# Sums of squares moved to VectorE, the norms' work in another order, and a pointwise product in three passes

## What is computed

```python
x = layer_norm(ALPHA * x + gt1 * y, ln1_g, ln1_b)          # "l1"
h = x * (1.0 + sc2) + sh2
f = jnp.square(jax.nn.relu(h @ w_ff1)) @ w_ff2
x = layer_norm(ALPHA * x + gt2 * f, ln2_g, ln2_b)          # "l2"
# second block, even layer, for x and for the context:
h = rmsnorm(x, e_norm) * (1 + scale) + shift               # "en"
a_val, a_glu, a_gate, b_val, b_gate = split(h @ e_w_in)
u = a_val * sigmoid(a_glu)
u = silu(layernorm(dwconv(u, a_conv_w) + a_conv_b))
y_a = (u @ a_pw_w + a_pw_b) * silu(a_gate)                 # the pointwise product
y_b = fourier_mix(b_val, b_fw) * silu(b_gate)
x = x + gate * (concat(y_a, y_b) @ e_w_out)
```

## Time and profile before

| | |
|---|---|
| median of 3 runs (lowest, highest) | 2692.74 us (2689.59, 2699.69) |
| the profiled execution's own time, and its span | 2691.15 us, 2689.3 us |
| busy: TensorE, VectorE | 2496.9 us (93%), 1397.6 us (52%) |
| busy: GpSimd, ScalarE | 732.4 us (27%), 610.2 us (23%) |
| mean granted TensorE clock | 0.966 of full speed |

### The profile page before, as it was taken

How to read it: one execution, slowest core, us unless ns; L and a number is a source line. 1 busy time by engine, 2 the same in 40 slices (tenths; PEclk the granted TensorE clock), 3 DMA queues, 4 the chain that set the end, 5 groups by cost and what they waited for, 6 DMA issues and landing times.

```text
span 2689.3 us, 29003 instructions
## 1 busy us (share of the span) xinstructions
PE 2496.9 (93%) x11544; PEld 1946.7 (72%) x11544; DVE 1397.6 (52%) x1577; ACT 610.2 (23%) x882; POOL 732.4 (27%) x490
## 2 busy tenths in 40 slices
PE   5998779989999999999998689999998999999998
PEld 3876556657678888888886468886586778878877
DVE  7556743434643444444435779996528321336633
ACT  3002224431422001101123421113204210023311
POOL 1241320015462332332345211210045223340011
PEclk9999879999999999999999899999999999999999
DMA  6651000022232332332222121112232531110021
GB/s 225 200 162 61 20 18 8 8 95 86 59 106 83 95 98 75 94 98 88 80 84 80 38 94 42 34 39 102 70 122 82 160 78 47 47 40 1 1 86 71
DMA packets 228851, 206.96 MB, mean 77 GB/s; under 512 B 15248, under 2 KB 203280, under 8 KB 227712
## 3 DMA queue, kind: packets, MB, share of 16 engines
q1 hardware_dynamic: 223552, 178.61, 22.0%
q10 hardware_dynamic: 3840, 21.89, 2.1%
q0 software_dynamic: 1344, 4.91, 0.5%
HBM read 180.35 MB, written 17.83 MB: 74 GB/s over the span
## 4 chain that ended last, share of the span: by engine, by line
PE 79%; DVE 10%; issue 3%; ACT 3%; PEld 2%; POOL 1%; DMA 1%; PEldq 1%; ACTq 0%; DVEq 0%; SPq 0%; POOLq 0%
PE G L1633 28%; PE G L304 26%; PE M L3001 3%; PE G L1099 2%; PE M L307 2%; DVE WPT L3038 2%; PE G L2506 1%; PE M L2986 1%; PE M L400 1%; PE M L1649 1%; PE G L2322 1%; PE M L2322 1%; PE M L1010 1%; PE G L2349 1%; PE M L2508 1%
## 5 line engine op out<-in xcount | busy, mean ns | idle before, releaser
L278 POOL TENSOR_SCALAR WH<-RAW 128x1024 fp32r<-128x1024 f32 (+1 forms) x154 | 132.7, 861 | 888.4 <-PE G L1633 516.2
L304 PE MATMUL G<-HH,WH 128*128 128x512 f32 x1056 | 337.3, 400 | 14.7 <-POOL WL L2164 7.8
L304 PE MATMUL G<-HH,WL 128*128 128x512 f32 x1056 | 332.9, 396 | 0.0
L304 PE MATMUL G<-HL,WH 128*128 128x512 f32 x1056 | 332.8, 396 | 0.0
L281 POOL TENSOR_TENSOR WL<-RAW,WH 128x1024 fp32r<-128x1024 f32 (+1 forms) x154 | 299.4, 1944 | 12.9
L1633 PE MATMUL G<-HH,WH 128*128 128x512 f32 x640 | 227.2, 404 | 13.5 <-POOL WL L281 8.7
L304 PEld LDWEIGHTS G<-HH,WH 128*128 128x128 f32 x1056 | 188.6, 189 | 61.6 <-issue 19.5
L1633 PE MATMUL G<-HH,WL 128*128 128x512 f32 x640 | 223.7, 398 | 0.0
L1633 PE MATMUL G<-HL,WH 128*128 128x512 f32 x640 | 223.7, 398 | 0.0
L304 PEld LDWEIGHTS G<-HL,WH 128*128 128x128 f32 x1056 | 188.8, 188 | 42.4
L304 PEld LDWEIGHTS G<-HH,WL 128*128 128x128 f32 x1056 | 188.9, 188 | 42.2
(11 more groups left out here) (536 smaller groups left out, 4430.5 us busy)
## 6 DMA issues: line engine op xcount, KB each, us to landing
RAW<-in_w_ff SPq DMA_DIRECT2D x40, 512.0 KB, 3.9
RAW<-in_w_ff SPq DMA_DIRECT2D x80, 256.0 KB, 2.7
WVEC<-in_w_ada SPq DMA_DIRECT2D x24, 512.0 KB, 4.7
FVEC<-in_e_w_mod SPq DMA_DIRECT2D x24, 512.0 KB, 3.9
FVEC<-in_o_w_mod SPq DMA_DIRECT2D x24, 512.0 KB, 3.7
RAW<-in_o_w_in SPq DMA_DIRECT2D x24, 512.0 KB, 3.6
RAW<-in_e_w_in SPq DMA_DIRECT2D x20, 512.0 KB, 3.5
ADA<-in_w_ada SPq DMA_DIRECT2D x4, 2048.0 KB, 19.6
```

What stands on the lines that cost most here:

```text
L278: pool.tensor_scalar(hi, raw, 1.0, 0.0, ALU.mult, ALU.add).then_inc(w_high, 1)
L304: m = pe.matmul(G[s][:, n * w:(n + 1) * w], part[s][:, k, :], acts[i][:, k, n * w:(n + 1) * w], start=first, stop=last)
```

## The change

1. **Sums of squares.** For half 0 and half 1 of l1, and half 0 of l2, seven additions on VectorE (`squares_add`) sum the squares into HNR, and TensorE does one matmul with ones in place of eight, one unit later than before (after ("o", 0, 3, 1), ("a", 0, 3, 0) and ("a", LAST, 3, 1)). A square on ScalarE now waits for an addition, where it waited for a matmul. Half 1 of l2, the last one, keeps its eight matmuls (`last_var_pe`).
2. **Orders of the norms.** In l1 half 1 `root` stands behind the fourth `feed`. At the end of `wf` the matmul `en_sum_pe(0)` stands one unit later; the emptying of b4 to b7 and `center("l2", 1)` come ahead of the rms norm of half 0; and ScalarE's `en_tile(f, 0)` stands behind `second_finish(f, 1)` of the same f, where two of them were done ahead.
3. **Pointwise product.** U and UC are split: ScalarE copies each tile behind its SiLU (UH, UHC), GpSimd subtracts (UL, ULC). The weights of the four units are split by GpSimd, and TensorE does three passes.
4. **X comes back later.** UH lies where tiles 0 to 3 of X came back, so these too are fetched at the start of `eo`: one transfer of 2 MB for tiles 0 to 3, one for tiles 4 to 7, both behind XC.
5. **`ein`.** GpSimd makes both parts of units 2 and 3 as well.
6. **Odd layer.** SWAPW (64 KB) is fetched ahead of two tables, where it was fetched behind them.

```diff
 def norm_var_pe(pe, tag, h):
+    pe.wait_ge(S(tag + "_va"), 7 * h + 7)
+    pe.matmul(M[1][:, half(h)], ONES[:], HNR[h][:], start=True, stop=True).then_inc(S(tag + "_var"), 1)
...
 def squares(tag, h):
     for f in range(KT):
         g = KT * h + f
         act.wait_ge(S(tag + "_c"), g + 1)
-        if g >= 2:
-            act.wait_ge(S(tag + "_squ"), g - 1)
+        if h and f < 2:
+            act.wait_ge(S(tag + "_va"), 6 + f)
+        elif f >= 2 and tag == "l2" and h:
+            act.wait_ge(S("l2_squ"), f - 1)
+        elif f >= 2:
+            act.wait_ge(S(tag + "_va"), 7 * h + max(f - 2, 1))
...
+def squares_add(tag, a, b, h):
+    sq = HSQ2 if tag == "l2" else HSQ
+    for f in range(a, b):
+        dve.wait_ge(S(tag + "_sq"), KT * h + f + 1)
+        if f > 1:
+            dve.wait_ge(S(tag + "_va"), 7 * h + f - 1)
+        dve.tensor_tensor(HNR[h][:], sq[0][:] if f == 1 else HNR[h][:], sq[f % 2][:], ALU.add)\
+           .then_inc(S(tag + "_va"), 1)
...
 # ef_act
     act.activation(u[:, j, 0:T], u[:, j, 0:T], ACT.Silu, ...).then_inc(S("ea_s"), 1)
+    act.wait_ge(S("ea_s"), 4 * i + j + 1)
+    act.activation((UH, UHC)[i][:, j, :], u[:, j, 0:T], ACT.Copy).then_inc(S("ea_h"), 1)
...
 # ef_pe
+    for i, (part, a) in enumerate(((WH, UH[:, k, :]), (WH, UL[:, k, 0:SEQ]), (WL, UH[:, k, :]))):
...
+def ef_pool(pool):
+    gate(pool, current[0])
+    for i, (u, _, _, T) in enumerate(sums_of):
+        for j in range(4):
+            pool.wait_ge(S("ea_h"), 4 * i + j + 1)
+            pool.tensor_tensor((UL, ULC)[i][:, j, 0:T], u[:, j, 0:T], (UH, UHC)[i][:, j, :].bitcast(F32),
+                               ALU.subtract).then_inc(S("ea_l"), 1)
+    for j in range(N_PW):
+        split_one(pool, info("ef")["r0"] + len(dft_raw) + j, info("ef")["u0"] + j, 4)
...
 # eo_act
-    for f in range(4, KT):
-        act.dma_start(X[:, f, :], SPILL[:, f, :]).then_inc(x_late, 16)
+    for f, back in ((0, x_first), (4, x_late)):
+        act.dma_start(X[:, f:f + 4, :], SPILL[:, f:f + 4, :]).then_inc(back, 16)
```

More of the change, by code:

```diff
@@ L2020, in wf_dve @@
             rms_add(KT - 1, 0)
[L2021 to L2024 removed]
+            for f in range(4, KT):
+                evict_ff(("b", LAST, f, 1))
+                gather_ff(f, 1)
+            center("l2", 1)
             en_inverse(0)
[L2026 to L2027 removed]
             en_scaled(0, 0)
[L2029 to L2031 removed]
+            inverse("l2", 1)
+            scaled("l2", 0, 1)
             en_scaled(1, 0)
             en_low(0, 0)
[L2034 to L2037 removed]
             context_low()
@@ L2340, in ef_pe @@
             for j in range(N_PW):
-                pe.wait_ge(raw_loaded[j % 2], 16 * ((r0 + j) // 2 + 1))
+                U_ = info("ef")["u0"] + j
+                pe.wait_ge(w_split[j % 2], U_ // 2 + 1)
+                pe.wait_ge(unit_freed[j % 2], U_ // 2)
                 if j == 0:
-                    pe.wait_ge(S("ea_s"), 8)
+                    pe.wait_ge(S("ea_l"), 8)
                     pe.wait_ge(S("ef_y"), 6)
-                if j >= 2:
-                    pe.wait_ge(S("ep_g"), 2 * (j - 1))
                 for k in range(4):
-                    for n in range(2):
-                        pe.matmul(G[j % 2][:, n * 512:(n + 1) * 512], RAW[j % 2][:, k, :],
-                                  U[:, k, n * 512:(n + 1) * 512], start=(k == 0), stop=(k == 3))
+                    for i, (part, a) in enumerate(((WH, UH[:, k, :]), (WH, UL[:, k, 0:SEQ]),
+                                                   (WL, UH[:, k, :]))):
+                        for n in range(2):
+                            pe.matmul(G[j % 2][:, half(n)], part[j % 2][:, k, :], a[:, half(n)],
+                                      start=(k == 0 and i == 0), stop=(k == 3 and i == 2))
                 if j == 0:
@@ L2353, in ef_pe @@
                 for k in range(4):
-                    m = pe.matmul(M[j % 2][:, 0:CTX], RAW[j % 2][:, k, :], UC[:, k, 0:CTX], start=(k == 0), stop=(k == 3))
-                m.then_inc(raw_used[j % 2], 1)
+                    for i, (part, a) in enumerate(((WH, UHC[:, k, :]), (WH, ULC[:, k, 0:CTX]),
+                                                   (WL, UHC[:, k, :]))):
+                        m = pe.matmul(M[j % 2][:, 0:CTX], part[j % 2][:, k, :], a, start=(k == 0 and i == 0),
+                                      stop=(k == 3 and i == 2))
+                m.then_inc(unit_done[j % 2], 1)
         def ef_done(eng, g):
@@ L2475, in ef_dve @@
                 dve.sem_inc(S("ep_lo"), 1)
-        stage("ef", dict(act=ef_act, pe=ef_pe, dve=ef_dve, sp_free=ef_sp), raw=[((len(dft_raw) + N_PW) // 2, None)],
-              dmas=[(X[:, f, :], SPILL[:, f, :]) for f in range(4)])
+        def ef_pool(pool):
[7 more added lines that the diff above has]
+                split_one(pool, info("ef")["r0"] + len(dft_raw) + j, info("ef")["u0"] + j, 4)
+        stage("ef", dict(act=ef_act, pe=ef_pe, dve=ef_dve, sp_free=ef_sp, pool=ef_pool),
+              raw=[((len(dft_raw) + N_PW) // 2, None)], units=N_PW)
         EO = [(f, n) for n in range(2) for f in range(KT)]
```

93 lines of the change are left out of this document (43 added, 50 removed).

## The result

| | median | runs | range |
|---|---|---|---|
| before | 2693.79 us | 6 | 2689.59 to 2699.69 |
| after | 2714.26 us | 6 | 2711.31 to 2721.55 |

What follows compares the result with a forecast made beforehand. The prediction took TensorE to bound the kernel on average (79% of the chain), but VectorE at most edited places. Terms summed to +10.6 us on 2691.15, giving 2701.8, predicted as 2702 us; own range 2693 to 2711, 8 in 10 2682 to 2718.

Steps and rivals of the forecast that it cites:

- l1, half 0: First half of norm l1: VectorE's additions blocked by GpSimd's subtractions make the reciprocal late; +3 us, bounds -2 and +5.
- l1, half 1: Second half of norm l1: TensorE waits for a1's bank, pays for the clock, reciprocal 2.5 us later; +1.5, bounds -2 and +4.
- l2 half 0 and the end of `wf`: Earlier mean and faster clock save 12.2 us, the longer loop costs more; +4 us, bounds 0 and +6.
- `ein`: Unit 2's weights come earlier because GpSimd makes both parts; -4.9 us, bounds -5 and 0.
- `ef`: Pointwise units shorten by 6.4 us, but weight splits, copies and a wait before "c" cost more; +3, bounds -1.6 and +5.
- `eo`: First X tiles queue behind XC, so TensorE waits 3.3 us plus up to 1.84 for the clock; +4, bounds 0 and +15.
- SWAPW's term: Odd layer: fetching SWAPW first changes nothing, as all three are awaited and bytes are equal; 0, bounds -1 and +1.
- The other side, -12.2: End of wf with l2 half 0: 9.4 us from earlier starts, plus 1.0 and 1.84 us from a fast clock.
- a new gap of over 3 us: TensorE's clock anywhere: such a wait drops it to 1.2 GHz and costs some 1.84 us on top.
- rival 3: In eo the 2 MB X transfer lands at 1976, costing 14 us instead of 4: 2712 us; chance 0.18.
- Rival 1: Whole kernel: TensorE's saved time comes through, 31 us, giving 2660 us; chance 0.10.
- Rival 2: Whole kernel: additions slip between GpSimd's subtractions, pauses stay short, X is home in time: 2687 us; chance 0.17.

Runs made afterwards that it cites:

- the row of ein: Kernel before, with GpSimd also splitting the weights of units 2 and 3 of that stage, nothing else changed: 2684.9 us, ratio 0.9966.
- norms2: Kernel before with VectorE's sums of squares, l1 half 1's variance sum back after unit a2 and a1 emptied between squares: 2701.2 us, ratio 1.0028.
- tail2: Kernel before with l2 half 1's centering moved early at the end of wf, en tiles still two ahead in the loop: 2688.1 us, ratio 0.9976.
- tail: Kernel before with only the new order at the end of wf: early centering, en tiles one ahead instead of two: 2701.8 us, ratio 1.0034.
- pw: Kernel before with only the three-pass pointwise product, its copies and splits, and X back in two 2 MB transfers: 2708.9 us, ratio 1.0056.
- best: Kernel before plus GpSimd's ein split, early centering with tiles two ahead, three-pass product with copies behind evictions, X in three transfers: 2678.6 us, ratio 0.9935.
- fill: The kernel best plus 14 idle matmuls in TensorE's wait after the second scores of the odd layer's attention: 2672.6 us, ratio 0.9914.
- pw2: Kernel before with the three-pass product and 2 MB transfers, ScalarE's UH and UHC copies behind the EV and EVC evictions: 2692.8 us, ratio 0.9995.

## Why the forecast came out half as large

The sign of the whole and the places of the waits were right, the sum was half. By its terms, with what the profiled pair measured:

| term | forecast | measured |
|---|---|---|
| l1, half 0 | +3 | +3.8 |
| l1, half 1 | +1.5 | +4.7 |
| l2 half 0 and the end of `wf` | +4 | +9.0 |
| `ein` | -4.9 | -5.0 |
| `ef` | +3 | +3.2 |
| `eo` | +4 | +3.6 |
| sum | +10.6 | +19.3 |
| not in the sum: clock in untouched stretches | 0 | +5.8 |

The sum of 19.3 is close to the +20.5 of the medians, the 25.1 is of one pair of executions. SWAPW's term, 0, is in none of the rows, and nothing contradicts it. For `eo` the stretch up to the context's sum is taken; the 1.6 us behind it are also in the row of ein, which doesn't touch `eo`.

*Half 1 of l1 is the first mis-sized term*, past its upper bound of +4. The wait of 4 to 5 us (5.14) and the half clock came as written, but the clock cost a3 2.5 us (8.62 for 6.14) and not 1.84. So a3, which I let end "about 1 us earlier than before", ended 0.7 us later (26.0 us behind the mean instead of 25.2); and the variance, moved behind it, made the reciprocal come at 28.6 us instead of 22.7, so 5.9 later, where I had 2.5. TensorE paid for it ahead of unit b2, with a wait of 3.92 us that I had left out: b2 needs the bank of b0, which VectorE empties behind that reciprocal (742.94 to 743.68). `norms2` shows both halves of it: with the old placing +4.7 falls to +1.9, that 3.92 us is gone, and the rest is the clock and the wait for the additions.

*The end of `wf` is the second*, past its +6. The loop was right to the tenth: from the end of the variance to the second `en_sum` it took 15.9 us more, where 12.0 + 2.3 + 1.5 were forecast. The other side, -12.2, was not: the mean of half 1 came 6.7 us sooner, not 9.4, and of the 2.84 us of a fast clock behind it only the 0.96 of the pair came; the variance took 9.40 us as before. I had put its slow start down to the long gaps ahead of it (3.50 and 5.48 us) and let it go with them. They went, the clock was at 1.00 from 1486 to 1502, and still it fell behind the two short waits of 1.79 and 1.45 us, so that the window from 1506 shows 0.62. So "a new gap of over 3 us" was too simple a rule. `tail2` shows what there was to gain, 6.6 us, and that the loop cost all the rest.

*Right:* `ein` to 0.1 us; `ef` by its steps (wait 5.73 for 6.2, units 6.97 for 7.00, the split's 1.38 for 1.6, UC's scaling behind GpSimd); `eo`, where the first 2 MB made the addition wait 4.53 us and it ran 18.5 us behind `eo`'s first matmul (1978.58 - 1960.13), where the forecast had 19.9 and rival 3 28.5. TensorE's own wait there was 1.93 us, not 3.3, and a stretch at half clock close behind it cost the other 1.7. By its time, 2712, rival 3 would look like the winner, but its 14 us in `eo` did not come. Rival 1 fell with the page: TensorE's share fell, its busy time didn't. Rival 2 fell at every place but `ein`, where it had the forecast's term; in l1's half 0 five additions were held.

*Missed altogether:* what a shift does to the clock of stages that are not touched. The largest piece is the attention, +8.05 us in the profiles of after, `tail`, `pw` and `best`, about 0 in seven others and in the kernel before. `fill` shows what sets it off: the wait of 3.75 us at its start lets the clock fall. Small matmuls follow, and whether they are what keeps it down was not tested. What decides whether it is back in 7 to 14 us or in 27 to 31 is open: the start of the attention doesn't sort them (slow at 2373.6, 2393.2, 2399.1, 2403.2; quick at 2374.2, 2390.8, 2397.5, 2398.0). Nor is it shown how many of the six timed executions of the changed kernel had it; 19.3 us by its own places against a median of +20.5 leaves room for little.

## What to carry to other kernels

Matmuls that stand beside another engine's chain cost nothing when they are there, and may cost when they go: TensorE then waits, and runs what follows at half clock. Take work off TensorE only where its timeline shows no wait behind it, and otherwise leave it, or try idle matmuls in the wait, which helped at the one wait where it was tried. In a loop through three engines count how many tiles each is ahead: one fewer made each turn 1.5 us longer here, seven turns over. And where one profiled pair is explained, look at the stretches that nothing touched first; theirs is the size of what the pair can't tell.

## What the runs showed of the hardware that I had not expected

- After a wait of 3.75 us at full clock, with small matmuls behind it, TensorE stayed at 1.2 GHz for 27 to 31 us in four kernels, although it was then busy 10.00 of 10 us, and for 7 to 14 us in nine others with the same code, the kernel before among them; 14 idle matmuls (3.48 us) in the wait kept it at 2.4 GHz.
- The same instructions with the same waits ran at a clock of 1.00 in one kernel and 0.83 in another for 10 us; untouched stretches differed by 1.5 to 8 us from one profile to the next. Six executions of `best` spread over 15 us and six of `fill` over 4, so the spread seems to come in good part from one such place.
- At the end of `wf` the clock fell (1.00 from 1486 to 1502, 0.62 from 1506 to 1510) though the longest gaps in between were two waits of 1.79 and 1.45 us around one pair of matmuls.
- VectorE operations that read one input from a TensorE bank pass beside GpSimd's subtraction at 0.69 us, while one with both in SBUF took 3.20 instead of 1.23. GpSimd's copy holds VectorE up too: two additions beside it took 1.35 and 1.52 us for 0.69.
- With 512 KB as the first transfer in place of 2 MB, the first addition to X waited 0.74 us in place of 5.77 (`best` and `pw2`).
